# Seven block products in place of eight in the MLP output product of a two-layer encoder, and narrower passes in its input product

## The chip, the cores and the metric

The kernel runs on one core of one Trainium2 chip. The metric is the device time of one execution in microseconds (us), the median of several runs. One execution was taken with the profiler.

## The reference

Two layers of an encoder over 256 tokens of width 1024, in float32. Each layer has two kinds of attention, a gated mix and an MLP. The part that matters here is the MLP:

```python
h = rms_norm(x, g_mlp_pre)
h = jnp.square(jax.nn.relu(h @ w_mlp_in)) @ w_mlp_out      # 1024 -> 4096 -> 1024
x = x + rms_norm(h, g_mlp_post)
```

## The kernel before

**Products in three passes.** A float32 product on TensorE (PE) is made of three passes: each operand is split into a high part (cast to float32r) and a low part (the rest). `high*high`, `high*low` and `low*high` are added in a PSUM bank. The weights are split in the kernel as they arrive: the scalar engine (ACT) casts a piece into `w_hi` (`hi`, line 678), the vector engine (DVE) subtracts it from the loaded data into `w_lo` (`lo`, line 1019), and PE uses both. A piece is half a load, 1024 elements per partition. Pieces live in a ring of four (`RING`): the cast of piece p waits until PE has used piece p - 4 (`piece_used`), and PE waits for `lo_ready`. The loads go through the queue of SyncE (SP) into four slots of `raw`; a slot is loaded again when DVE has split its last piece.

**The MLP.** The 4096 hidden columns are worked in 8 chunks of 512. Chunk 0's input product is `first_product`, chunk 1's `turned_product` (256-column passes, lines 1455 to 1457). From chunk 2 on it is `mlp_in_wide`, which gives the hidden columns on partitions: for each block of 128 hidden columns and each 128 rows of the weights one pass of 512 columns (high weights times high and low activations side by side in `s1_both`, line 1698) and one of 256 (low weights, line 1701). The two halves of a bank are then added by DVE (`sum_h`, `tensor_reduce`, line 1067) into `relu_h`; ACT does the relu in place (line 784); GpSimd (POOL) squares it into `tok` (`square`, line 531); ACT and DVE split that into the stationary operand `s2_hi`, `s2_lo` (lines 792 and 1058).

The output product (`mlp_out`, and `product` with lines 1380 to 1382) takes chunk j's 512 rows of `w_mlp_out` in four pieces. For each piece, token tile (2 of 128) and block of 128 rows it issues three passes of 512 columns: 48 passes per chunk. The sums of all chunks stay in the four banks `acc`, one for each token tile and half of the 1024 output columns. `finish` is the product of chunk 7, ordered by token tile so that the norm of tile 0 can start early.

**Order.** Per layer PE runs: `first_product`, `turned_product` for chunk 1, output product of chunk 0, then a loop of five (input product of chunk j + 2, output product of chunk j + 1), then the input product of chunk 7, the output product of chunk 6 and `finish`. All engines follow a hand-written program order with semaphores.

Of the kernel before, what the change touches and what calls it, by code (L numbers as in the profile page):

```python
# [65 lines left out]
    + [("out", 4, COL)] * 4 + [("mlp", 4, COL)] * 32)  # L66
NL = len(LOADS)
NP = 2 * NL
# [4 lines left out]
L_LOOP = L_MLP + 6  # L73
LOOP_J = MJ - 3
assert NL == 64 and LOADS[L_MLP][0] == "mlp" and LOADS[L_MLP - 1][0] == "out"

# [7 lines left out]
def piece_rows(p):  # L84

    nk = LOADS[p // 2][1]
    cut = (nk + 1) // 2
    return (0, cut) if p % 2 == 0 else (cut, nk)
# [77 lines left out]
def build(nc, x_d, pos_d, g_mix_pre, g_mix_post, g_mlp_pre, g_mlp_post, w_in, b_gate, sinks_d, q_norm,  # L166
          kv_norm, w_uq, w_ukv, w_oa, w_ob, w_out, w_mlp_in, w_mlp_out, out_d):
    ctx = ExitStack()
    with ctx:
# [101 lines left out]
        h_summed = sem("h_summed")  # L271
# [30 lines left out]
        def raw_view(p):  # L302

            n, N = p // 2, LOADS[p // 2][2]
            k0, k1 = piece_rows(p)
            return raw[:, n % RAW, k0 * N:k1 * N]

        def in_order(p, *views):

            if LOADS[p // 2][0] != "ukv":  # L310
                return views
# [4 lines left out]
        def split_view(buf, p):  # L316
            k0, k1 = piece_rows(p)
            return buf[:, p % RING, 0:(k1 - k0) * LOADS[p // 2][2]]
# [32 lines left out]

        h_banks = sc + tp
# [30 lines left out]
        def _(sp):  # L383
# [8 lines left out]
            def raw_free(pos, n):  # L392

                sp.wait_ge(lo_ready, pos.count(NP, 2 * n + 2, 8))
# [9 lines left out]
            for l in range(DEPTH):  # L404
# [56 lines left out]
                mlp_out(pos, n + 4, 0)  # L461
                with sp.Fori(0, LOOP_J) as j:
                    here = Pos(l, j)
                    mlp_in(here, L_LOOP, j + 2)
                    mlp_out(here, L_LOOP + 2, j + 1)
                n = L_LOOP + 4 * LOOP_J
                mlp_in(pos, n, MJ - 1)
                mlp_out(pos, n + 2, MJ - 2)
                mlp_out(pos, n + 4, MJ - 1)
                assert n + 6 == NL  # L470
# [11 lines left out]
        def _(pool):  # L482
# [41 lines left out]
            def square(pos, j):  # L524

                for t in range(TT):
                    pool.wait_ge(relu_done, pos.count(TT * MJ, TT * j + t + 1, TT))
                    if j > 1:

                        pool.wait_ge(h_split, pos.count(TT * (MJ - 1), TT * (j - 2) + t + 1, TT))  # L530
                    g.tensor_tensor(tok[:, t, 0:COL], relu_h[:, t, :], relu_h[:, t, :], ALU.mult).then_inc(h_ready, 1)  # L531
# [37 lines left out]
            for l in range(DEPTH):  # L569
# [69 lines left out]
                square(pos, 0)  # L639
                square(pos, 1)  # L640
                with pool.Fori(0, LOOP_J) as j:
                    square(Pos(l, j), 2)
                square(pos, MJ - 1)
# [6 lines left out]
        def _(act):  # L650
# [15 lines left out]
            def hi(pos, upto):  # L666

                while state[0] <= upto:
                    p = state[0]
                    n = p // 2  # L670
# [1085 lines left out]
```

## Time and profile before

| | |
|---|---|
| median of 3 runs | 753.39 us (753.14 to 753.55) |
| the profiled execution | 753.48 us |
| its span, first to last instruction | 751.5 us |
| PE, matmul busy | 740.3 us, 99% of the span |
| DVE busy | 505.8 us, 67% |
| ACT busy | 414.4 us, 55% |
| POOL busy | 158.6 us, 21% |
| HBM read | 130.59 MB, 175 GB/s over the span |

A share is an average over stages, and a matmul is counted with its pipeline, so that overlapping ones make PE look full. The distance from one start to the next tells what a pass costs. In the timeline a row gives start, duration, engine, line, operation and operands; `x2` means that two like instructions were merged, and the bracket at the end tells how long the engine was idle before it and who ended that.

### The profile page before, as it was taken

The numbers are of one execution on the slowest core, as the hardware profiler recorded it, in microseconds if no ns is written. First come the engines' busy times: TensorE is split into PE (matmuls) and PEld (weight loads), VectorE is DVE, ScalarE is ACT, GpSimd is POOL, SyncE is SP. The second block draws the span as 40 slices with busy tenths as digits, with TensorE's granted clock in tenths as the row PEclk, the third lists the DMA queues.
The fourth block names the chain that finished last, engine by engine and source line by source line (L and its number), as shares of the span: only waits on it lengthen the run. The fifth ranks groups of instructions, "written<-read, shape, count | busy, mean of one in ns | idle before, by whom it ended". The sixth has DMA issues, their size and how long they took to land.

```text
span 751.5 us, 11313 instructions
## 1 busy us (share of the span) xinstructions
PE 740.3 (99%) x4194; PEld 640.3 (85%) x4194; DVE 505.8 (67%) x678; ACT 414.4 (55%) x779; POOL 158.6 (21%) x262
## 2 busy tenths in 40 slices
PE   8999999999999999999999999999999999999996
PEld 7999887888798888888889997888888988888885
DVE  5878777567765656656686887766668566565674
ACT  6867665434664544444576866644447444554452
POOL 1990433000130111110128414220003210011110
PEclk9999999999999999999999999999999999999999
DMA  7866633565465545466338584335473656555511
GB/s 260 208 205 218 220 113 115 167 215 168 129 215 178 213 170 193 156 207 211 105 114 242 182 281 144 113 117 194 139 223 121 220 164 223 189 202 176 202 71 56
DMA packets 79501, 132.19 MB, mean 176 GB/s; under 512 B 15290, under 2 KB 21476, under 8 KB 79204
## 3 DMA queue, kind: packets, MB, share of 16 engines
q1 hardware_dynamic: 79188, 131.64, 53.7%
q8 instruction: 26, 0.43, 0.2%
q14 instruction: 15, 0.12, 0.0%
q10 hardware_dynamic: 272, 0.00, 0.0%
HBM read 130.59 MB, written 1.05 MB: 175 GB/s over the span
## 4 chain that ended last, share of the span: by engine, by line
PE 91%; DVE 3%; ACT 2%; POOL 1%; DMA 1%; issue 1%; SPq 0%; POOLq 0%; ACTq 0%; DVEq 0%
PE acc L1380 15%; PE acc L1382 15%; PE acc L1381 15%; PE tp L1698 6%; PE sc L1698 6%; PE acc L1414 4%; PE tp L1355 3%; PE tp L1701 3%; PE sc L1701 3%; PE sc L1516 2%; PE sc L1457 2%; PE sc L1455 2%; PE sc L1456 2%; PE sc L1380 2%; PE sc L1381 1%; PE sc L1382 1%
## 5 line engine op out<-in xcount | busy, mean ns | idle before, releaser
L1019 DVE TENSOR_TENSOR w_lo<-raw,w_hi 128x1024 fp32r<-128x1024 f32 (+4 forms) x256 | 306.0, 1216 | 162.5 <-ACT w_hi L678 161.0
L678 ACT CAST w_hi<-raw 128x1024 fp32r<-128x1024 f32 (+4 forms) x256 | 251.5, 997 | 177.7 <-PE acc L1382 94.3
L1380 PE MATMUL acc<-w_hi,s_hi 128*128 128x512 f32 x288 | 112.2, 390 | 0.0
L1381 PE MATMUL acc<-w_lo,s_hi 128*128 128x512 f32 x288 | 112.1, 389 | 0.0
L1382 PE MATMUL acc<-w_hi,s_lo 128*128 128x512 f32 x288 | 112.0, 389 | 0.0
L1380 PE MATMUL acc<-w_hi,s_both 128*128 128x512 f32 (+2 forms) x256 | 95.5, 373 | 0.0
L1382 PE MATMUL acc<-w_hi,s_both 128*128 128x512 f32 (+2 forms) x256 | 93.4, 365 | 0.0
L1381 PE MATMUL acc<-w_lo,s_both 128*128 128x512 f32 (+2 forms) x256 | 93.3, 364 | 0.0
L531 POOL TENSOR_TENSOR tok<-relu_h 128x512 f32<-128x512 f32 x32 | 37.0, 1161 | 263.6 <-ACT relu_h L784 241.6
L1382 PEld LDWEIGHTS acc<-w_hi,s_lo 128*128 128x128 f32 x288 | 54.1, 188 | 11.3
L1380 PEld LDWEIGHTS acc<-w_hi,s_hi 128*128 128x128 f32 x288 | 54.1, 188 | 10.8
L1381 PEld LDWEIGHTS acc<-w_lo,s_hi 128*128 128x128 f32 x288 | 54.1, 188 | 10.6
L1698 PE MATMUL tp<-s_both,w_hi 128*128 128x512 f32 x192 | 60.3, 395 | 0.0
L1698 PE MATMUL sc<-s_both,w_hi 128*128 128x512 f32 x192 | 60.2, 395 | 0.0
L802 ACT ACTIVATE probs<-sc,neg_m 128x128 f32<-128x128 f32 (+2 forms) x96 | 35.2, 390 | 40.0 <-DVE neg_m L1137 22.0
L1382 PEld LDWEIGHTS acc<-w_hi,s_both 128*128 128x128 f32 x256 | 48.2, 188 | 7.8
L1380 PEld LDWEIGHTS acc<-w_hi,s_both 128*128 128x128 f32 x256 | 48.2, 188 | 7.4 <-DVE w_lo L1019 0.4
L1381 PEld LDWEIGHTS acc<-w_lo,s_both 128*128 128x128 f32 x256 | 48.3, 189 | 6.9
L514 POOL TENSOR_TENSOR var<-sums,norm_k 128x1 f32<-128x1 f32 x24 | 8.5, 354 | 186.9 <-ACT squares L740 186.7
L1701 PEld LDWEIGHTS tp<-s_both,w_lo 128*128 128x128 f32 x192 | 36.1, 188 | 8.5
L1701 PEld LDWEIGHTS sc<-s_both,w_lo 128*128 128x128 f32 x192 | 36.1, 188 | 8.4
L784 ACT ACTIVATE relu_h<-relu_h 128x512 f32<-128x512 f32 x24 | 15.2, 632 | 44.0 <-DVE relu_h L1067 44.0
(212 smaller groups left out, 1337.6 us busy)
## 6 DMA issues: line engine op xcount, KB each, us to landing
raw<-in_w_mlp_in SPq DMA_DIRECT2D x32, 1024.0 KB, 5.3
raw<-in_w_mlp_out SPq DMA_DIRECT2D x32, 1024.0 KB, 5.0
raw<-in_w_in SPq DMA_DIRECT2D x24, 1024.0 KB, 5.3
raw<-in_w_oa SPq DMA_DIRECT2D x8, 1024.0 KB, 5.0
raw<-in_w_out SPq DMA_DIRECT2D x8, 1024.0 KB, 5.0
raw<-in_w_ob SPq DMA_DIRECT2D x4, 1024.0 KB, 4.9
raw<-in_w_in SPq DMA_DIRECT2D x3, 768.0 KB, 4.9
raw<-in_w_in SPq DMA_DIRECT2D x4, 576.0 KB, 6.5
```

Source lines behind the costliest of these rows:

```text
L531: g.tensor_tensor(tok[:, t, 0:COL], relu_h[:, t, :], relu_h[:, t, :], ALU.mult).then_inc(h_ready, 1)
L678: s.copy(high, src).then_inc(hi_ready, 1)
L784: s.activation(relu_h[:, b, :], relu_h[:, b, :], ACT.Relu).then_inc(relu_done, 1)
L802: ins = s.activation(probs[:, i % 2, a * w:(a + 1) * w], sc[i % 2][:, a * w:(a + 1) * w], ACT.Exp, bias=neg_m[:, c + a:c + a + 1], scale=S ...
L1019: v.tensor_tensor(low, src, high, ALU.subtract).then_inc(lo_ready, 1)
L1355: ins = nc.tensor.transpose(b[0:rows, i * P:(i + 1) * P], src, ident[:, :])
L1380: mm(banks[t][:, 0:N], h[:, kk, tk], wh[:, k, :], start=(start and k == 0), stop=False)
L1381: mm(banks[t][:, 0:N], h[:, kk, tk], wl[:, k, :], start=False, stop=False)
L1382: ins = mm(banks[t][:, 0:N], low[:, kk, tk], wh[:, k, :], start=False, stop=(stop and k == b - a - 1))
L1414: ins = mm(acc[t][:, 0:N], xs[:, 2 * i + k, t * P:(t + 1) * P], w[:, k, :], start=(first and i == 0 and k == 0), stop=(last and i == 3 and ...
L1698: mm(bank[:, :].rearrange("p (a n) -> p a n", a=2), wh[:, k, cols], s1_both[:, :, 2 * i + k, :], start=(i == 0 and k == 0), stop=False)
L1701: ins = mm(bank[:, SEQ:2 * SEQ], wl[:, k, cols], s1_hi[:, 2 * i + k, :], start=False, stop=(i == 3 and k == 1))
```

## The change

For chunks 1 to 6 the output product is done in the Strassen-Winograd way. A half chunk has two blocks of 128 hidden rows; with the two token tiles and the two halves of the output columns it is a product of 2 x 2 by 2 x 2 blocks, eight block products. The change makes seven, from sums of the blocks, in seven PSUM banks (`acc` 0 to 3, `sc` 0 and 1, `tp` 0), each with three passes of 512 columns.

- POOL makes the sums of the activations (`square_and_sum`: two squares of 256 elements, four sums of 128) and of the weights (`weight_sums`: a difference of 1024 elements, two of 512, into the gate buffers, two halves ahead).
- A half chunk has six weight pieces: `in0` and `in1` (1024 elements each), `low` (1024), `first` (512), `t13` and `t24` (1024 each, of the sums).
- The seven banks are combined once per layer on DVE (`add_bank`, seven additions of 512), before the output product of chunk 0, which now comes after chunks 1 to 6. Chunk 7 stays last.
- The input product of chunks 2 to 7 goes in blocks of 128 hidden columns (`in_piece`), 24 passes of 256 columns each, all three kinds of pass into the same 256 columns of a bank; the relu reads that bank (`relu_of`), so `sum_h` goes away. Its loads have rows of 256 columns, those of the output weights whole rows of 1024.
- The loops over chunks are written out.

```diff
-    + [("out", 4, COL)] * 4 + [("mlp", 4, COL)] * 32)
+    + [("out", 4, COL)] * 4 + [("mlp", 4, COL)] * 4 + [("in", KD, SEQ), ("pair", 2, D)] * 12 + [("mlp", 4, COL)] * 4)
...
+def half_order(s):
+    if s == 0:
+        return ("in0", "in1", "low", "first", "t13", "t24")
+    if s == NHALF - 1:
+        return ("in0", "low", "first", "t13", "t24", "in1")
+    return ("in0", "low", "first", "in1", "t13", "t24")
...
             def raw_free(pos, n):
-                sp.wait_ge(lo_ready, pos.count(NP, 2 * n + 2, 8))
+                upto = LAST_PIECE[n - RAW] + 1 - (NP if n < RAW else 0)
+                sp.wait_ge(lo_ready, pos.count(NP, 2 * RAW + upto))
...
+            def relu_ready(pos, j, b):
+                if j < 2:
+                    pool.wait_ge(relu_done, pos.count(2 * TT, TT * j + b + 1))
+                else:
+                    pool.wait_ge(h_relued, pos.count(2 * NHALF, 2 * (2 * (j - 2) + b) + 2))
+                if j > 1:
+                    pool.wait_ge(h_split, pos.count(TT * (MJ - 1), TT * (j - 2) + b + 1))
+            def square_and_sum(pos, j, b):
+                relu_ready(pos, j, b)
+                tile = tok[:, b, :].rearrange("p (s n) -> p s n", n=P)
+                ka = relu_h[:, b, 0:SEQ].rearrange("p (t n) -> p t n", t=TT)[:, ::-1, :]
+                kb = relu_h[:, b, SEQ:2 * SEQ].rearrange("p (t n) -> p t n", t=TT)
+                g.tensor_tensor(tile[:, 0:2, :], ka, ka, ALU.mult)
+                sums_a.link(g.tensor_tensor(tile[:, 2:4, :], kb, kb, ALU.mult))
+                g.tensor_tensor(tile[:, 7, :], tile[:, 1, :], tile[:, 0, :], ALU.subtract)
+                sums_a.link(g.tensor_tensor(tile[:, 5, :], tile[:, 0, :], tile[:, 3, :], ALU.add))
+                sums_a.link(g.tensor_tensor(tile[:, 6, :], tile[:, 5, :], tile[:, 1, :], ALU.subtract))
+                g.tensor_tensor(tile[:, 4, :], tile[:, 2, :], tile[:, 6, :], ALU.subtract).then_inc(h_ready, 1)
+            def weight_sums(pos, s):
+                n = L_PAIR + 2 * s + 1
+                loads, in_layer = transfers(n)
+                pool.wait_ge(raw_full[n % RAW], pos.count(16 * in_layer, 16 * loads))
+                if s >= 2:
+                    pool.wait_ge(lo_ready, pos.count(NP, 2 * RAW + half_piece(s - 2, "t24") + 1))
+                block = raw[:, n % RAW, :].rearrange("p (i n) -> p i n", i=4)
+                made = t_buf[s % 2].rearrange("p (i n) -> p i n", i=4)
+                at = lambda i: pos.count(3 * NHALF, 3 * s + i)
+                g.tensor_tensor(made[:, 0:2, :], block[:, 1::2, :], block[:, 0:2, :], ALU.subtract).then_inc(t_made, 1)
+                pool.wait_ge(t_made, at(1))
+                g.tensor_tensor(made[:, 2, :], block[:, 3, :], made[:, 0, :], ALU.subtract).then_inc(t_made, 1)
+                pool.wait_ge(t_made, at(2))
+                g.tensor_tensor(made[:, 3, :], block[:, 2, :], made[:, 2, :], ALU.subtract).then_inc(t_made, 1)
...
+                for t in range(TT):
+                    square(pos, 0, t)
+                sums_a.pos, sums_a.n = pos, 0
+                weight_sums(pos, 0)
+                for b in range(2):
+                    square_and_sum(pos, 1, b)
+                weight_sums(pos, 1)
+                for s in range(NHALF):
+                    j, b = half_of(s)
+                    if j < MJ - 1:
+                        square_and_sum(pos, j, b)
+                    else:
+                        square(pos, j, b)
+                    if s + 2 < NHALF:
+                        weight_sums(pos, s + 2)
...
+                    elif part in ("t13", "t24"):
+                        act.wait_ge(t_made, pos.count(3 * NHALF, 3 * ((n - L_PAIR) // 2) + (1 if part == "t13" else 3)))
...
+            def relu_of(pos, s, f):
+                j, b = half_of(s)
+                used(pos, half_piece(s, f"in{f}"))
+                act.wait_ge(h_ready, pos.count(TT * MJ, TT * (j - 1) + b + 1))
+                nc.scalar.activation(relu_h[:, b, f * SEQ:(f + 1) * SEQ], in_bank(s, f)[:, 0:SEQ], ACT.Relu).then_inc(h_relued, 1)
...
+                for half in range(1, NHALF - 1):
+                    p = P_PAIR + 6 * half
+                    relu_of(pos, half, 0)
+                    hi(pos, p + 4)
+                    pair_high(pos, *half_of(half - 1))
+                    hi(pos, p + 6)
+                    relu_of(pos, half, 1)
+                    hi(pos, p + 9)
...
-            def sum_h(pos, j, p):
...
+            def pair_low(pos, j, b):
+                dve.wait_ge(h_hi, pos.count(TT * (MJ - 1), TT * (j - 1) + b + 1))
+                v.tensor_tensor(pair_lo[b], tok[:, b, P:D], pair_hi[b].bitcast(F32), ALU.subtract).then_inc(h_split, 1)
...
+                for half in range(1, NHALF - 1):
+                    p = P_PAIR + 6 * half
+                    lo(pos, p + 4)
+                    pair_low(pos, *half_of(half - 1))
+                    lo(pos, p + 6)
+                    lo(pos, p + 9)
...
+                def in_piece(pos, s, f):
+                    p, bank = half_piece(s, f"in{f}"), in_bank(s, f)
+                    pe.wait_ge(lo_ready, pos.count(NP, 2 * RAW + p + 1))
+                    if s > 0:
+                        pe.wait_ge(h_relued, pos.count(2 * NHALF, 2 * s + f))
...
+                    for k in range(KD):
+                        mm(out, wh[:, k, :], s1_hi[:, k, :], start=(k == 0), stop=False)
+                        mm(out, wh[:, k, :], s1_lo[:, k, :], start=False, stop=False)
+                        ins = mm(out, wl[:, k, :], s1_hi[:, k, :], start=False, stop=(k == KD - 1))
+                    ins.then_inc(piece_used, 1)
...
+                for half in range(1, NHALF - 1):
+                    in_piece(pos, half, 0)
+                    pair_low(pos, half)
+                    pair_first(pos, half)
+                    in_piece(pos, half, 1)
+                    pair_t13(pos, half)
+                    pair_t24(pos, half)
...
+                def whole(c):
+                    return lambda t: pe.wait_ge(combined, pos.count(7, (1, 4, 6, 7)[2 * c + t]))
+                for i in range(4):
+                    product(pos, P_LAST + i, 0, s2, pair[i // 2], free=whole(i // 2) if i % 2 == 0 else None, seeded=True)
```

## Rows read from the trace of the kernel before

**Rows 1.** Page: busy per engine; granted clock in 40 slices; the chain by engine.

```profile
PE 740.3 (99%) x4194; PEld 640.3 (85%) x4194; DVE 505.8 (67%) x678; ACT 414.4 (55%) x779; POOL 158.6 (21%) x262
...
PEclk9999999999999999999999999999999999999999
...
PE 91%; DVE 3%; ACT 2%; POOL 1%; DMA 1%; issue 1%; SPq 0%; POOLq 0%; ACTq 0%; DVEq 0%
```

**Rows 2.** Timeline of PE: start us, duration us, the starts that bound the products.

```profile
222.89 0.40 PE L1380 MATMUL acc<-w_hi,s_hi 128*128 128x512 f32 x1
...
233.80 0.39 PE L1698 MATMUL sc<-s_both,w_hi 128*128 128x512 f32 x1
...
244.94 0.40 PE L1380 MATMUL acc<-w_hi,s_hi 128*128 128x512 f32 x1
...
365.96 0.39 PE L1380 MATMUL acc<-w_hi,s_hi 128*128 128x512 f32 x1
```

**Rows 3.** Timeline of PE: first and last of runs without a gap.

```profile
210.51 0.28 PE L1455 MATMUL sc<-s_both,w_hi 128*128 128x256 f32 x1
...
216.15 0.28 PE L1457 MATMUL sc<-s_both,w_lo 128*128 128x256 f32 x1
...
228.13 0.39 PE L1382 MATMUL acc<-w_hi,s_lo 128*128 128x512 f32 x1
```

**Rows 4.** Timeline of DVE: three low parts back to back.

```profile
209.13 3.50 DVE L1019 TENSOR_TENSOR w_lo<-raw,w_hi 128x1024 fp32r<-128x1024 f32 x3 [1.95 <-ACT w_hi L678]
```

**Rows 5.** ACT in 222 to 372 by shape (busy us, mean ns), and one timeline row.

```profile
L678 ACT CAST w_hi<-raw 128x1024 fp32r<-128x1024 f32 x53 | 55.0, 1049 | 51.8 <-PE acc L1382 26.8 <-PE tp L1701 25.0
L792 ACT CAST s_hi<-tok 128x512 fp32r<-128x512 f32 x14 | 8.0, 616 | 0.0
...
223.09 1.09 ACT L778 ACTIVATE relu_h<-sc 128x512 f32<-128x512 f32 x2 [1.78 <-PE sc L1457]
```

**Rows 6.** Single lines of POOL: duration ns min/median/max, first and last start, forms.

```profile
L531 POOL TENSOR_TENSOR tok<-relu_h x32: 1041/1042/2022, 211.6 to 727.2; 128x512 f32<-128x512 f32 x32
...
L590 POOL TENSOR_TENSOR latent<-latent,rstd x8: 616/1070/1591, 29.4 to 401.3; 128x384 f32<-128x384 f32 x4, 128x256 f32<-128x256 f32 x4
...
L600 POOL TENSOR_TENSOR gate_a<-cost,rstd x4: 395/402/1386, 37.8 to 403.5; 128x128 f32<-128x128 f32 x4
```

**Rows 7.** Timeline of DVE and POOL where low parts meet squares.

```profile
211.41 1.22 DVE L1019 TENSOR_TENSOR w_lo<-raw,w_hi 128x1024 fp32r<-128x1024 f32 x1
...
211.56 1.96 POOL L531 TENSOR_TENSOR tok<-relu_h 128x512 f32<-128x512 f32 x1 [2.31 <-ACT relu_h L778]
...
212.95 1.66 DVE L1019 TENSOR_TENSOR w_lo<-raw,w_hi 128x1024 fp32r<-128x1024 f32 x1 [0.32 <-ACT w_hi L678]
...
213.49 2.02 POOL L531 TENSOR_TENSOR tok<-relu_h 128x512 f32<-128x512 f32 x1
...
214.73 1.85 DVE L1019 TENSOR_TENSOR w_lo<-raw,w_hi 128x1024 fp32r<-128x1024 f32 x1
...
224.77 1.04 POOL L531 TENSOR_TENSOR tok<-relu_h 128x512 f32<-128x512 f32 x1
...
225.15 1.74 DVE L1019 TENSOR_TENSOR w_lo<-raw,w_hi 128x1024 fp32r<-128x1024 f32 x1 [2.58 <-ACT w_hi L678]
```

**Rows 8.** DVE with one operand in PSUM: beside a square, and a line's durations.

```profile
247.03 0.68 DVE L1067 TENSOR_REDUCE relu_h<-tp 128x256 f32<-128x512 f32 x1
...
247.35 1.04 POOL L531 TENSOR_TENSOR tok<-relu_h 128x512 f32<-128x512 f32 x1 [21.54 <-ACT relu_h L784]
...
L1111 DVE TENSOR_TENSOR s_lo<-acc,s_hi x8: 668/680/695, 101.1 to 488.5; 128x512 fp32r<-128x512 f32 x8
```

**Rows 9.** Window of an output product: length, PE, PEld, DVE, ACT, POOL busy, clock.

```profile
244.90:256.00 11.10, 11.10 (x51) 9.22 (x50) 7.28 (x8) 5.27 (x6) 2.08 (x2) 1.00 0.49 182
```

**Rows 10.** Page, DMA issues: count, KB each, median us from issue to landing.

```profile
raw<-in_w_mlp_in SPq DMA_DIRECT2D x32, 1024.0 KB, 5.3
...
raw<-in_w_in SPq DMA_DIRECT2D x4, 512.0 KB, 4.2
```

More of the change, by code:

```diff
@@ L270, in build @@
         relu_done = sem("relu_done")
-        h_summed = sem("h_summed")
+        h_relued = sem("h_relued")
+        h_step = sem("h_step")
+        t_made = sem("t_made")
+        p1_copied = sem("p1_copied")
+        combined = sem("combined")
         h_ready = sem("h_ready")
@@ L302, in raw_view @@
         def raw_view(p):
-            n, N = p // 2, LOADS[p // 2][2]
+            n, part = PIECES[p]
+            kind, nk, N = LOADS[n]
+            if kind == "in":
+                cols = slice(0, P) if part == "in0" else slice(P, 2 * P)
+                return raw[:, n % RAW, :].rearrange("p (k n) -> p k n", k=KD)[:, :, cols]
+            if kind == "pair":
+                s = (n - L_PAIR) // 2
+                return {"low": raw[:, n % RAW, D:2 * D], "first": raw[:, n % RAW, 0:COL],
+                        "t13": t_buf[s % 2][:, 0:D], "t24": t_buf[s % 2][:, D:2 * D]}[part]
             k0, k1 = piece_rows(p)
@@ L1705, in h_is_split @@
-                def h_is_split(pos, j):
-                    pe.wait_ge(h_split, pos.count(TT * (MJ - 1), TT * j, TT))
-                def mlp_out(pos, p, start=False):
-                    for i in range(4):
-                        product(pos, p + i, 0, s2, pair[i // 2], start and i % 2 == 0)
+                def in_piece(pos, s, f):
[3 more added lines that the diff above has]
+                        pe.wait_ge(h_relued, pos.count(2 * NHALF, 2 * s + f))
+                    wh, wl = (split_view(w, p).rearrange("p (k n) -> p k n", k=KD) for w in (w_hi, w_lo))
+                    out = bank[:, 0:SEQ]
+                    for k in range(KD):
[3 more added lines that the diff above has]
+                    ins.then_inc(piece_used, 1)
@@ new lines, in pair_piece @@
+                def pair_piece(pos, s, name, terms):
+                    p, b = half_piece(s, name), s % 2
+                    pe.wait_ge(lo_ready, pos.count(NP, 2 * RAW + p + 1))
+                    wh, wl = (split_view(w, p).rearrange("p (i n) -> p i n", n=COL) for w in (w_hi, w_lo))
+                    first, last = s == 0, s == NHALF - 1
+                    for i, (a, bank) in enumerate(terms):
+                        tk = slice(SUM_A[a] * P, (SUM_A[a] + 1) * P)
+                        mm(bank[:, :], pair_hi[b][:, tk], wh[:, i, :], start=first, stop=False)
+                        mm(bank[:, :], pair_hi[b][:, tk], wl[:, i, :], start=False, stop=False)
+                        ins = mm(bank[:, :], pair_lo[b][:, tk], wh[:, i, :], start=False, stop=last)
+                    ins.then_inc(piece_used, 1)
@@ new lines, in pair_low, with pair_first, pair_t13, pair_t24 @@
+                def pair_low(pos, s):
+                    pe.wait_ge(h_split, pos.count(TT * (MJ - 1), s + 1))
+                    pair_piece(pos, s, "low", (("a12", acc[0]), ("s4", acc[2])))
+                def pair_first(pos, s):
+                    pair_piece(pos, s, "first", (("a11", sc[0]),))
+                def pair_t13(pos, s):
+                    pair_piece(pos, s, "t13", (("s1", acc[3]), ("s3", tp[0])))
+                def pair_t24(pos, s):
+                    pair_piece(pos, s, "t24", (("s2", sc[1]), ("a22", acc[1])))
```

274 lines of the change are left out of this document (144 added, 130 removed).

## The prediction

> **What bounds the kernel now.** I read the page's busy shares, its chain and the clock row first, then the timeline of the MLP stage. PE is busy for 99% of the span at full granted clock, and 91% of the chain that ended last is PE [rows 1]. So the MLP stage has no slack on PE. I mark it off by two starts in the first layer: the last input product of chunk 1 ends where the first 512-column pass of the output product starts, at 222.89, and `finish`, the output product of chunk 7, starts at 365.96 [rows 2]. Between them lie 143.1 us, all PE. The profiled execution took 753.48 us (its span is 751.5), against a median of 753.39 for the runs, so I add differences to 753.4.
>
> **PE, pass by pass.** A 512-column pass follows the last after 0.227 us (228.13 to 233.80, 25 steps) and a 256-column pass after 0.120 us (210.51 to 216.15, 47 steps) [rows 2, 3]. The narrow pass costs 6.5 ns more than half a wide one. The input product of a chunk is now 32 passes of 512 and 32 of 256, 32 x 0.227 + 32 x 0.120 = 11.1 us (233.80 to 244.94 in the trace [rows 2]). After the change it is 96 passes of 256: 11.52 us, 0.38 more. The output product of a half chunk drops from 24 passes to 21, which gives 3 x 0.227 = 0.68. Over 6 chunks (12 halves) and two layers: 24 x 0.68 = 16.3 gained, 12 x 0.38 = 4.6 lost, net 11.7 us on PE alone. A half (input and output product of 256 hidden columns) then costs PE 48 x 0.120 + 21 x 0.227 = 10.5 us, where half a chunk costs 11.0 now.
>
> The Trainium skill (TensorE: Matmul & The Clock Gate, section "Wait — 56ns, not 53.3ns?") gives back-to-back passes a fixed 2.5 ns over their columns at 2.4 GHz; the rows have 13.5. By the page the narrow passes would cost almost nothing and the gain on PE would be about 14.5 us; the measured pitches decide.
>
> **What the other engines must do for it.** Per half, DVE now has 4 low parts of 1024 elements, one low part of h (512) and two reductions out of PSUM. After: five low parts of 1024 (`in0`, `in1`, `low`, `t13`, `t24`), one of 512 (`first`), and `pair_low` with 896. All seven read two SBUF operands. Back to back a 1024 costs 1.14 (three in 3.50, the last one 1.22 long) [rows 4], so DVE needs 5 x 1.14 + 0.61 + 1.0 = 7.3 us of a half. ACT casts a piece in 1.05 and 512 elements in 0.62 [rows 5]; five pieces, `first`, 896 elements of h and two relus of 256 (0.4 each, an estimate from the 1.09 of two relus of 512) make 7.6. Both are below 10.5, and by themselves would stay hidden.
>
> POOL squares 512 elements per half now (1.04 us). After the change it squares 2 x 256, makes four sums of 128 for the activations, and for the weights a difference of 1024 and two of 512. Its durations alone are 1.04 for 512, 0.62 for 256 and 0.40 for 128 [rows 6], a slope of 1.67 ns per element, so a 1024 takes 1.9. Sum: 1.9 + 2 x 1.04 + 2 x 0.62 + 4 x 0.40 = 6.8 us. Also below 10.5.
>
> **But DVE and POOL don't run side by side.** This is the step that decides. In [rows 7] a POOL square that takes 1.04 alone took 1.96 and 2.02 while DVE made low parts, and the low parts, 1.22 alone, took 1.66 and 1.85. Read the ends: DVE 212.63, POOL 213.52, DVE 214.61, POOL 215.51, DVE 216.58. Each instruction finishes a fixed time after the end of the other engine's: 0.90 for the POOL 512, 1.08 for the DVE 1024. One pair takes 1.98 us, the sum of both. The row at 225.15 says it again: DVE waits for the POOL square to end at 225.81 and ends 1.08 later. DVE instructions that read one SBUF operand and PSUM don't wait: the reduction at 247.03 keeps its 0.68 while POOL keeps its 1.04 [rows 8]. That is why the loop of before never shows it: POOL's squares fall beside the reductions there, and POOL is busy only 2.08 us per chunk [rows 9].
>
> No row has a POOL subtraction of this size beside a DVE low part. I count all nine of POOL's, because its multiplications of other shapes and operands stretched in the same way, the 0.62 to as much as 1.59 and the 0.40 to 1.39 [rows 6]. If only the two squares counted, the shared time of a half would be under 8 us; that is rival (a).
>
> The Trainium skill (SBUF — State Buffer, section "Who interferes with whom") says that a DVE instruction with two SBUF inputs and any GpSimd instruction that reads SBUF exclude each other for the whole instruction. By that rule all nine count; no run here shows it for them yet.
>
> **The sum of a half.** Held by DVE: 5 x 1.08 + 0.55 + 0.95 = 6.9. Held by POOL, 0.90 for 512 with the same slope: 1024 1.75, two 512 1.80, two 256 0.95, four 128 1.04, together 5.5. That is 12.4 us if one always follows the other at once. The upper bound is both engines' stand-alone times end to end, 7.3 + 6.8 = 14.1; the lower one gives POOL nothing but its slope, 3072 elements at 1.67 ns, 5.1, beside DVE's 6.9: 12.0. POOL's linked steps leave short holes that DVE can't always use, so I take 12.75, near the lower of the two sums because both queues have work waiting. PE's 10.5 is below all three: it will stand about 2.2 us in each half, most of it at `low` or `t13`, for `lo_ready`. The ring of four pieces lets PE run through single blockages; it can't carry a steady deficit.
>
> **A layer.** Start: after 222.89 the two first input pieces give PE 5.8 us. In that time chunk 1 must be relued (to 224.2 in the trace [rows 5]), squared and summed by POOL (2.8 alone, with waits for DVE's next pieces about 5), cast and subtracted (2 us), so `low` of half 0 starts about 3 us late. Half 1 is saturated, with its `weight_sums` behind the sums of both halves of chunk 1: 30 us for the first two halves (27 to 34). Nine more at 12.75: 114.8. The last half and the product of chunk 0 are PE again, since POOL has no weight sums left: 10.5 + 10.9, and 0.6 for handovers: 22. The seven additions of the banks are hidden: DVE takes 0.68 for 512 elements with one operand in PSUM [rows 8], and four of the seven, 2.7, must be done before tile 1 of the first piece, and the last input piece and tile 0 give them 2.9 + 1.4 us. Sum 30 + 114.8 + 22 = 166.8 against 143.1: 23.7 more, 47 for both layers. Forecast: 753.4 + 47.4 = **801 us**.
>
> **The new waits.** ACT's cast of `t13` and `t24` waits for POOL (`t_made`); behind it on ACT stand `pair_high`, the relu of `in1` and the next casts, and so DVE and PE. POOL makes these sums two halves ahead (`weight_sums(s + 2)`), so the wait costs only if POOL is a whole half late, rival (b). `relu_of` waits for `h_ready` two halves back, with the same lead. PE's wait for `h_relued` before an input piece has two or three pieces of other products in between, 1.9 us at least, against a relu of 0.4: nothing. On SP the load of the pair waits until `t24` is split, instead of being freed when its own data is read; behind it is only the next load.
>
> Transfers stay hidden. The two loads of a half have 1 KB and 4 KB rows. 512 KB in 1 KB rows lands after 4.2 us, 1 MB in 2 KB rows after 5.3 [rows 10]; even twice 4.2 and once 5.3 end to end is 13.7, with the fixed time of a transfer counted thrice, and the slot of a load is free more than a half ahead.
>
> **The rivals.** (a) *Faster: the exclusion doesn't bind.* It decides from the point where DVE and POOL together hold less than PE's 10.5. Then PE is the bound, 12 x 10.5 + 10.9 = 137 per layer, plus 1 to 3 us at the start: 743 to 748, say **745**. For it: neither engine alone is above 7.3. Against it: the lock-step ends of [rows 7], and even the lower bound of 12.0 is above 10.5. Chance 0.09. (b) *The exclusion binds, but POOL also becomes late by its own order:* each linked step waits for a whole DVE instruction, and `weight_sums` stands behind the sums of h. A half then goes to 14.1: 34 + 127 + 23 = 184 per layer, **835**. Against it: DVE has only seven instructions per half to stand in the way, and both results are needed a half later. Chance 0.11. (c) *The granted clock falls in the stalls.* It is at its full 2.4 GHz in every slice of before [rows 1], but no slice there has a stall of 2.2 us in every 13. At the other level, 1.2 GHz, the columns of a pass would take twice as long: 48 x 0.227 + 21 x 0.440 = 20.1 us for PE's half, an estimate, and some 970 in all. Chance 0.03.
>
> **How the numbers follow.** The main case has 0.75: 12.0 to 13.7 per half with 27 to 32 at the start gives 780 to 823. 0.02 is for the exclusion binding only just, near 753. The range 780 to 827 leaves out (a), (c), the case near 753 and the dearer half of (b), 0.2 together. Faster by over 0.2% 0.09, within 0.2% (1.5 us, about what can be told from no change) 0.02, slower 0.89.
>
> **What would show it.** Right: in the halves, low parts of 1.7 us and longer and POOL subtractions of twice 1.04 and longer, ends in lock step; DVE and POOL busy near 100% of the stage; PE waiting for `w_lo`; pitch of halves about 12.7. Wrong: low parts at 1.22 beside POOL, and PE dense at 10.5 per half. If PE waits for a transfer or `relu_h`, the cause is another one.

## The result and the profile after

| | before | after |
|---|---|---|
| runs, median (lowest to highest), us | 753.47 (753.14 to 753.57) | 827.84 (825.90 to 827.97) |
| profiled execution, its span, us | 753.48, 751.5 | 825.90, 824.1 |
| mean granted clock | 0.998 | 0.981 |

The ratio is 1.098, with an interval of 1.096 to 1.100. The forecast was 801 with a range of 780 to 827, so the direction and the mechanism came out, but the size did not: 74 us slower, not 47, and 0.8 above the upper end of the range. The profiled execution is the fastest of the four; the tables below are read from it.

The page of after, busy time by engine, DVE, POOL and the granted clock in tenths over 40 slices, and the chain by engine:

```profile
PE 753.7 (91%) x4506; PEld 655.9 (80%) x4506; DVE 643.7 (78%) x692; ACT 457.1 (55%) x853; POOL 450.7 (55%) x454
DVE  5778777577679798988686878766686889888994
POOL 2971421001799999994037423300039999999910
PEclk9999999999999899999999999999999899999999
PE 55%; POOL 30%; DVE 10%; ACT 3%; issue 2%; POOLq 0%; ACTq 0%; DVEq 0%
```

Against [rows 1], PE falls from 99% to 91% of the span, and the chain of work that ended last now runs through POOL for 30% and DVE for 10%; before, it was 91% PE. POOL is near full through both MLP stages, and otherwise only in one slice near the start, where it also was before. The clock row has its first 8s.

The stage of the first layer, by four starts on PE (us, duration): the first input piece of half 0, the one of half 2, the one of half 11, and the output product of chunk 7. The last column is the idle time before and who ended it:

```profile
222.55 0.28 PE L1844 MATMUL tp<-s_both,w_hi 128*128 128x256 f32 x1
253.54 0.39 PE L1844 MATMUL tp<-s_both,w_hi 128*128 128x256 f32 x1 [0.57 <-DVE w_lo L1149]
379.87 0.39 PE L1844 MATMUL tp<-s_both,w_hi 128*128 128x256 f32 x1 [0.57 <-DVE w_lo L1149]
402.00 0.39 PE L1524 MATMUL acc<-w_hi,yb_hi 128*128 128x512 f32 x1
```

It lasts 179.45 us, where [rows 2] had 143.07 (365.96 - 222.89). That is 36.4 more, and twice that, 72.8, is the whole difference of the spans (72.6). So nothing outside the two MLP stages moved: from the start of chunk 7's product in the first layer to the start of the stage in the second it is 225.62 us in both traces. Inside, by the terms of the prediction:

| term, per layer | forecast | measured |
|---|---|---|
| first two halves | 30 | 31.0 |
| nine halves, each | 12.75 | 14.04 (126.33 in all) |
| last half and the product of chunk 0 | 22 | 22.1 |

The nine halves alone hold the miss: 9 x 1.29 x 2 = 23 us of the 27.

The two windows below are those nine halves and one of them (length, then busy time and count of PE, weight loads, DVE, ACT and POOL, the granted clock, the DMA share, GB/s):

```profile
253.50:379.90 126.40, 104.21 (x622) 89.70 (x622) 110.86 (x64) 63.24 (x82) 122.87 (x82) 0.96 0.47 150
337.90:351.90 14.00, 11.11 (x70) 9.53 (x70) 12.06 (x8) 6.93 (x10) 13.61 (x10) 1.00 0.47 147
```

POOL is busy for 97% of them, against 2.08 us per chunk before [rows 9], and PE for 82%. The waits of the same stretch put it down to the low parts, with no transfer among them (engine, line, waited for: us in total, times, longest):

```profile
PEld sc L1858 <- DVE w_lo L1149: 22.6, 9, 3.1
PE sc L1858 <- DVE w_lo L1149: 18.8, 9, 2.6
```

L1858 with `sc` is the first pass of a half that uses `low`: one stall of 2.5 us in each of the nine halves (2.1 by PE's own row), where the prediction put about 2.2 for the whole half. The half has 3.5 above PE's 10.5; most of the rest is a second, short stall before an input piece.

**The lock-step and the term that was too small.** The timeline of DVE and POOL from `t13` of one half on, start and duration:

```profile
342.39 1.33 DVE L1149 TENSOR_TENSOR w_lo<-gate_a,w_hi 128x1024 fp32r<-128x1024 f32 x1 [0.61 <-ACT w_hi L791]
342.72 1.32 POOL L614 TENSOR_TENSOR tok<-tok 128x128 f32<-128x128 f32 x1
344.01 2.42 POOL L627 TENSOR_TENSOR gate_b<-raw 128x1024 f32<-128x1024 f32 x1
345.05 2.32 DVE L1186 TENSOR_TENSOR s_lo<-tok,s_hi 128x896 fp32r<-128x896 f32 x1 [1.33 <-ACT s_hi L905]
346.50 2.00 POOL L629 TENSOR_TENSOR gate_b<-raw,gate_b 128x512 f32<-128x512 f32 x1
347.30 2.28 DVE L1149 TENSOR_TENSOR w_lo<-gate_a,w_hi 128x1024 fp32r<-128x1024 f32 x1
348.58 2.15 POOL L631 TENSOR_TENSOR gate_b<-raw,gate_b 128x512 f32<-128x512 f32 x1
349.50 2.31 DVE L1149 TENSOR_TENSOR w_lo<-raw,w_hi 128x1024 fp32r<-128x1024 f32 x1
350.69 1.59 POOL L609 TENSOR_TENSOR tok<-relu_h 128x256 f32<-128x256 f32 x1
```

Add start and duration and read the ends in order: DVE 343.72, POOL 344.04, POOL 346.43, DVE 347.37, POOL 348.50, DVE 349.58, POOL 350.73, DVE 351.81. Each ends a fixed time after the end before it, whoever had it: 1.08 for a DVE 1024 as forecast, 0.95 for `pair_low`; for POOL 0.32 for a 128, 2.39 for the 1024 (`weight_sums`, its difference of the raw blocks) and 1.13 to 1.15 for a 512. The forecast had 1.75 for that 1024 and 0.90 for a 512. Over the whole half, which ends 14.01 us after the last, DVE holds 6.9 (forecast 6.9) and POOL 7.1 (forecast 5.5). Their sum is the half: 14.0. No hole is left but the 0.08 us between two linked steps of POOL where DVE has nothing to do.

The POOL 1024 takes 2.42 from its start, with no DVE instruction in its way (DVE's next one, at 345.05, is the one that waits), where the slope taken from [rows 6] gave 1.9. All the instructions behind that slope read one tensor twice, or one tensor and a broadcast factor. Here the two operands are different data.

### The profile page after: what moved, and what is told of

It is laid out like the page before. It is cut to its first block, busy times and chain, and to the rows that moved or that the text cites. A ratio compares the mean times of both kernels' runs of the same rounds, so it can differ in the third digit from the quotient of the medians.

```text
span 824.1 us, 11845 instructions
## 1 busy us (share of the span) xinstructions
PE 753.7 (91%) x4506; PEld 655.9 (80%) x4506; DVE 643.7 (78%) x692; ACT 457.1 (55%) x853; POOL 450.7 (55%) x454
## 4 chain that ended last, share of the span: by engine, by line
PE 55%; POOL 30%; DVE 10%; ACT 3%; issue 2%; POOLq 0%; ACTq 0%; DVEq 0%
PE acc L1524 9%; PE acc L1527 9%; PE acc L1526 8%; DVE w_lo L1149 6%; PE acc L1559 4%; POOL tok L609 3%; POOL tok L610 3%; PE tp L1499 3%; POOL tok L612 3%; POOL gate_a L627 3%; POOL gate_b L627 2%; POOL tok L614 2%; POOL tok L611 2%; POOL gate_a L631 2%; POOL gate_b L631 2%; PE sc L1661 2%
## 5 line engine op out<-in xcount | busy, mean ns | idle before, releaser
L1149 DVE TENSOR_TENSOR w_lo<-raw,w_hi 128x1024 fp32r<-128x1024 f32 (+4 forms) x256 | 336.4, 1349 | 58.7 <-ACT w_hi L791 57.1
L1844 PE MATMUL tp<-s_both,w_hi 128*128 128x256 f32 x384 | 114.8, 299 | 14.3 <-DVE w_lo L1149 14.3
L1845 PE MATMUL tp<-s_both,w_hi 128*128 128x256 f32 x384 | 112.3, 292 | 0.0
L1846 PE MATMUL tp<-s_both,w_lo 128*128 128x256 f32 x384 | 112.1, 292 | 0.0
L1844 PEld LDWEIGHTS tp<-s_both,w_hi 128*128 128x128 f32 x384 | 77.3, 201 | 23.9 <-DVE w_lo L1149 22.8
L1845 PEld LDWEIGHTS tp<-s_both,w_hi 128*128 128x128 f32 x384 | 77.6, 202 | 1.0
L1846 PEld LDWEIGHTS tp<-s_both,w_lo 128*128 128x128 f32 x384 | 77.3, 201 | 0.0
L1149 DVE TENSOR_TENSOR w_lo<-gate_a,w_hi 128x1024 fp32r<-128x1024 f32 x24 | 45.4, 1899 | 11.4 <-ACT w_hi L791 11.4
L1149 DVE TENSOR_TENSOR w_lo<-gate_b,w_hi 128x1024 fp32r<-128x1024 f32 x24 | 44.4, 1850 | 11.3 <-ACT w_hi L791 11.3
L665 POOL TENSOR_TENSOR probs<-probs,denom 128x512 f32<-128x512 f32 x26 | 28.9, 1115 | 41.8 <-DVE denom L1235 41.8
L1186 DVE TENSOR_TENSOR yb_lo<-tok,yb_hi 128x896 fp32r<-128x896 f32 x12 | 28.4, 2370 | 12.9 <-ACT yb_hi L905 12.9
L1600 PE MATMUL sc<-s_both,w_hi 128*128 128x256 f32 x128 | 36.7, 287 | 0.0
```

The lines of the kernel that those rows point to most:

```text
L1149: v.tensor_tensor(low, src, high, ALU.subtract).then_inc(lo_ready, 1)
L1600: mm(out, wh[:, k, cols], s1_hi[:, kk, :], start=(i == 0 and k == 0 and f % 2 == 0), stop=False)
L1844: mm(out, wh[:, k, :], s1_hi[:, k, :], start=(k == 0), stop=False)
L1845: mm(out, wh[:, k, :], s1_lo[:, k, :], start=False, stop=False)
L1846: ins = mm(out, wl[:, k, :], s1_hi[:, k, :], start=False, stop=(k == KD - 1))
```

## The experiments

Each is timed beside the kernel before on the same chip (medians of it 753.34 to 753.40). "Half" means the time from one `in0` to the next in the first layer, "the start" what the first two halves cost beyond twice the later ones.

**Is it the weight sums on POOL?** `e1_no_wsums` drops POOL's three differences; `t13` and `t24` are split from the raw blocks instead, so two of the seven products have the wrong factor.

```diff
-                        "t13": t_buf[s % 2][:, 0:D], "t24": t_buf[s % 2][:, D:2 * D]}[part]
+                        "t13": raw[:, n % RAW, 0:D], "t24": raw[:, n % RAW, D:2 * D]}[part]
...
-                g.tensor_tensor(made[:, 0:2, :], block[:, 1::2, :], block[:, 0:2, :], ALU.subtract).then_inc(t_made, 1)
+                g.memset(made[:, 0, 0:1], 1.0).then_inc(t_made, 1)
```
(and the other two differences likewise)

> The changed kernel without POOL's three subtractions of the weights: t13 and t24 are split from the loaded data (so these two block products are computed with the wrong weights), POOL sets one element each instead. PE, ACT and DVE do the same work as in the changed kernel. Theory (a DVE low part and a POOL instruction that reads SBUF exclude each other): DVE holds 6.9 us of a half, POOL 2.4, together 9.3, below PE's 10.5; so halves of 10.5 to 10.8 us, low parts near 1.2 where no square is in the way, 744 to 752 us. Rival 1 (the time is lost to the clock of PE or to the order of the waits, not to POOL's reads): halves stay at 12 to 14 us, over 790 us.

Measured: 753.47, ratio 0.9994 (0.9984 to 1.0003). All 74 us are gone. The window of e1 over most of its halves:

```profile
250.00:355.00 105.00, 105.00 (x687) 96.34 (x686) 83.34 (x72) 70.14 (x91) 50.22 (x80) 1.00 0.58 190
```

PE is dense, POOL at 48%, and the halves are 10.56 each, 0.06 from the forecast of PE's cost. The three instructions are the cause of the slowdown. But the total is not the theory's 744 to 752: the start costs 5.1 us per layer (halves of 14.1 and 12.1), where rival (a) gave it 1 to 3. The place, on ACT, POOL and PE of e1:

```profile
231.78 1.33 POOL L614 TENSOR_TENSOR tok<-tok 128x128 f32<-128x128 f32 x1
233.14 0.94 ACT L905 CAST s_hi<-tok 128x896 fp32r<-128x896 f32 x1 [2.31 <-POOL tok L614]
233.99 3.46 ACT L791 CAST w_hi<-raw 128x1024 fp32r<-128x1024 f32 x4
234.71 0.39 PE L1860 MATMUL acc<-w_hi,yb_lo 128*128 128x512 f32 x1
237.04 0.39 PE L1844 MATMUL tp<-s_both,w_hi 128*128 128x256 f32 x1 [1.94 <-DVE w_lo L1149]
237.61 0.41 PE L1845 MATMUL tp<-s_both,w_hi 128*128 128x256 f32 x1
237.81 0.42 PE L1846 MATMUL tp<-s_both,w_lo 128*128 128x256 f32 x1
```

ACT stands 2.31 us in `pair_high(1, 1)` for POOL's last sum of half 1. The cast of `in0` of half 1 is queued behind it, and PE waits for that piece from 234.71 to 237.04. Two more things make up the 5.1: PE stood 1.3 us before `low` of half 0 (228.57 to 230.03), and after the stall at 237.04 its clock falls. From 237.61 on 16 narrow passes follow at 0.213 us instead of 0.120, which is 1.5 us; the window from 238 to 242 has a granted clock of 0.62. The ten runs of e1 show the price of that drop: from 750.68 at a mean clock of 0.999 to 753.84 at 0.994, twice 1.5 us apart.

**Does POOL's occupation hold DVE up, or its reading?** `e2_fill_only` leaves the sums out in the same way, and POOL fills the whole sum buffer three times instead, writing without reading.

```diff
-                g.tensor_tensor(made[:, 0:2, :], block[:, 1::2, :], block[:, 0:2, :], ALU.subtract).then_inc(t_made, 1)
+                g.memset(t_buf[s % 2][:, 0:4 * COL], 1.0).then_inc(t_made, 1)
```
(three times)

> As e1, but POOL fills the buffer of the sums three times (2048 elements each, linked as the subtractions were) in place of the subtractions; products as in e1. POOL writes as long as before, about 5.4 us per half, and reads nothing for it. Theory, exclusion through the reads alone: fills pass beside the low parts, halves of 10.5 to 11, 744 to 758 us. Rival 2, POOL's mere occupation or its writes are what DVE waits for: 6.9 + 2.4 + 5.4 = 14.7 us per half, 830 us or more.

Measured: 759.60, ratio 1.008 (1.007 to 1.010). The timeline:

```profile
298.04 1.80 POOL L627 MEMSET gate_b<- 128x2048 f32 x1
299.10 1.09 DVE L1186 TENSOR_TENSOR s_lo<-tok,s_hi 128x896 fp32r<-128x896 f32 x1 [1.33 <-ACT s_hi L905]
299.90 1.82 POOL L629 MEMSET gate_b<- 128x2048 f32 x1
300.11 2.35 DVE L1149 TENSOR_TENSOR w_lo<-raw,w_hi 128x1024 fp32r<-128x1024 f32 x2
```

Beside the fills `pair_low` takes 1.09 and two low parts take 2.35 together, what they take alone ([rows 4]: three in 3.50). POOL is busy for 92% of the window that e1 fills to 48%, and the halves are 11.03. So it is POOL's reads that DVE can't share; POOL being busy, and its writes, cost DVE nothing. The time above e1, and the miss of the expectation by 1.6, come from POOL's queue: the squares and sums of h stand behind 5.5 us of fills, and `low` comes about half a microsecond late in each half. Nine halves of 0.47 more in two layers are 8.5 us. Against e1's run without a clock drop, 750.68, e2 (clock 0.999) is 8.9 slower; against its median 6.1.

The Trainium skill (SBUF — State Buffer, section "Who interferes with whom") has the exclusion between a DVE instruction with two SBUF inputs and a GpSimd instruction that reads SBUF. It excepts a GpSimd instruction that only writes. The traces of after and of e2 agree: ends in strict turn with reads, 1.09 beside a fill.

**Why is POOL's share 7.1, not 5.5?** `e3_forms` keeps the sizes of the three weight instructions and changes their operands: the 1024 and the last 512 subtract a tensor from itself, the middle one multiplies two different ones. The weight sums are then not those of the reference.

```diff
-                g.tensor_tensor(made[:, 0:2, :], block[:, 1::2, :], block[:, 0:2, :], ALU.subtract).then_inc(t_made, 1)
+                g.tensor_tensor(made[:, 0:2, :], block[:, 0:2, :], block[:, 0:2, :], ALU.subtract).then_inc(t_made, 1)
...
-                g.tensor_tensor(made[:, 2, :], block[:, 3, :], made[:, 0, :], ALU.subtract).then_inc(t_made, 1)
+                g.tensor_tensor(made[:, 2, :], block[:, 3, :], made[:, 0, :], ALU.mult).then_inc(t_made, 1)
...
-                g.tensor_tensor(made[:, 3, :], block[:, 2, :], made[:, 2, :], ALU.subtract).then_inc(t_made, 1)
+                g.tensor_tensor(made[:, 3, :], block[:, 2, :], block[:, 2, :], ALU.subtract).then_inc(t_made, 1)
```

> The changed kernel with other operands for POOL's three weight instructions, all of the same size and place (the sums are then wrong, and with them two of the seven products): the 1024 subtracts one tensor from itself, the first 512 multiplies two tensors in place of a subtraction, the second 512 subtracts a tensor from itself. In the changed kernel POOL is alone from 344.04 to 346.43 with the 1024, which is 2.4 us where the forecast had 1.9, and a 512 ends 1.12 to 1.15 after DVE where the forecast had 0.90. Theory A, two different SBUF tensors as inputs cost POOL more: alone or from DVE's end, the 1024 takes 1.8 to 1.9, the multiplication 1.12 to 1.15, the last 512 0.9. Theory B, subtraction is dearer than multiplication: 2.4, 0.9, 1.15. Under A the half shortens by 0.5 to 0.8 us from 14.0.

Measured, one run: 810.85, halves of 13.24 in the stretch below (13.33 on average over nine). The timeline:

```profile
325.24 1.89 POOL L627 TENSOR_TENSOR gate_a<-raw 128x1024 f32<-128x1024 f32 x1
326.29 1.80 DVE L1186 TENSOR_TENSOR yb_lo<-tok,yb_hi 128x896 fp32r<-128x896 f32 x1 [1.33 <-ACT yb_hi L905]
327.21 2.01 POOL L629 TENSOR_TENSOR gate_a<-raw,gate_a 128x512 f32<-128x512 f32 x1
328.00 2.30 DVE L1149 TENSOR_TENSOR w_lo<-gate_b,w_hi 128x1024 fp32r<-128x1024 f32 x1
329.30 1.90 POOL L631 TENSOR_TENSOR gate_a<-raw 128x512 f32<-128x512 f32 x1
```

The subtraction of 1024 with one source takes 1.89, the 1.9 of the forecast. The one with one source of 512 ends at 331.20, 0.90 after DVE's 330.30. The multiplication of two sources ends at 329.22, 1.13 after DVE's 328.09. It is two different operands that cost, not the subtraction. These are theory A's numbers. The gain of a half, 0.77, is 2.42 - 1.89 and 1.14 - 0.90.

The trace of before had a row that says so, and the forecast passed it by. POOL's groups in its first 210 us (busy, mean ns):

```profile
L377 POOL TENSOR_TENSOR tok<-tok,gate_a 128x128 f32<-128x128 f32 x2 | 0.9, 460 | 0.2
```

It is 0.46 for 128 elements of two tensors, where [rows 6] have 0.40 with a factor that is broadcast. From 0.46 and 2.42 the slope is 1.96 / 896 = 2.19 ns per element; from one source it is 1.67.

The Trainium skill (GPSIMD Engine Reference, section "Elementwise — side-by-side cycle accounting") gives about 2.6 cycles per element at 1.2 GHz for `tensor_tensor` and calls it "the two-input RD-port floor"; that is 2.17 ns. With the 0.18 us that the 128 leaves over this slope as its fixed part, the POOL 1024 would be about 2.4, an estimate, and the trace agrees with its 2.42.

**What do the narrow passes cost by themselves?** `e4_narrow_input` is the kernel before, with the input product in passes of 256 and the relu read from the bank; it leaves nothing out.

```diff
-                                mm(bank[:, :].rearrange("p (a n) -> p a n", a=2), wh[:, k, cols], s1_both[:, :, 2 * i + k, :],
-                                   start=(i == 0 and k == 0), stop=False)
+                                mm(bank[:, 0:SEQ], wh[:, k, cols], s1_hi[:, 2 * i + k, :],
+                                   start=(i == 0 and k == 0), stop=False)
+                                mm(bank[:, 0:SEQ], wh[:, k, cols], s1_lo[:, 2 * i + k, :], start=False, stop=False)
...
-                    s.activation(relu_h[:, b, :], relu_h[:, b, :], ACT.Relu).then_inc(relu_done, 1)
+                        ins = s.activation(relu_h[:, b, f * SEQ:(f + 1) * SEQ], h_banks[2 * b + f][:, 0:SEQ], ACT.Relu)
```
(DVE's sum of the bank's two halves goes)

> The kernel before with the input product of chunks 2 to 7 in 256-column passes, three for each block, into one half of each bank, and the relu reading the bank; DVE's reductions go away. The second part of the change alone; pieces, loads and the output product are as before. Nothing is left out. By the pitches each chunk costs 0.38 us more on PE: 753.4 + 12 x 0.38 = 758.0 (757 to 759.5). Rival: the banks come free earlier and the relu is off DVE, which wins something back: 753 to 755.

Measured: 758.13, ratio 1.006 (1.005 to 1.008). 4.7 us slower, and 12 x 0.38 = 4.6 was the sum. The pitches of 0.227 and 0.120 hold, and what the rival hoped to win back isn't there.

The Trainium skill (TensorE: Matmul & The Clock Gate, section "Wait — 56ns, not 53.3ns?") gives a pass a fixed 2.5 ns over its columns. By that e4 would stand within 1 us of before, an estimate (4.6 x 1.25 / 6.5 = 0.9). It stands 4.7 above, and the measurement decides.

**Can the sums be had more cheaply?** `e5_wsums_dve` moves `weight_sums` from POOL to DVE, `e6_act_squares` also the squares of nine halves from POOL to ACT. Neither leaves anything out.

```diff
                     pair_low(pos, *half_of(half - 1))
                     lo(pos, p + 6)
+                    weight_sums(pos, half + 1)
                     lo(pos, p + 9)
...
+                if 0 < s < NHALF - 2:
...
+                    nc.scalar.activation(dst, part.rearrange("p (t n) -> p t n", t=TT), ACT.Square).then_inc(h_squared, 1)
```
(the added line at the top is e5, on DVE; the other two are e6, on ACT, behind the relu)

> The changed kernel with the three subtractions of the weights moved from POOL to DVE, in DVE's order behind the first low part of the next half. Nothing is left out. Theory: DVE holds 6.9 + 1.08 + 2 x 0.55 = 9.1 us, POOL 2.4: halves of 11.5 to 11.9 us, 770 to 785 us. Rival 3, no exclusion and DVE's queue as the bound: 7.3 + 2.4 = 9.7, below PE's 10.5, 745 to 750 us.

> As e5, and the squares of nine of the twelve halves are made by ACT behind the relu instead of by POOL. Nothing is left out. Theory: DVE 9.1 + POOL 1.5 (four sums of 128) = 10.6 us beside PE's 10.5: halves of 10.7 to 11.2 us, 748 to 762 us, close to the kernel before. Rival 3 gives 745 to 750 as for e5.

Measured: e5 773.53, ratio 1.027 (1.025 to 1.029); e6 762.35, ratio 1.012 (1.010 to 1.014). The window of e5:

```profile
254.00:370.00 116.00, 110.50 (x686) 97.24 (x685) 115.24 (x105) 72.98 (x92) 56.59 (x52) 1.00 0.56 187
```

DVE is busy for 99% of it, and the halves are 11.52, as the theory had it: 9.1 us for DVE and 2.4 for POOL's reads are 11.5, and the time lies in its range. So the sum of held times gives a half for a second division of the work, this time to 0.02. In e6 the halves come out at 10.56 and 11.26 in turn, 10.87 on average. That is close to PE's cost, but the total is 0.35 above the expected range and still 9 us above before.

**Can the start be saved?** `e7_early_in` is e1 (weight sums left out) with the next half's `in0` taken up ahead of `pair_high(1, 1)` and `pair_low(1, 1)`. `e8_early_both` does the same to e6, with the weight sums of half 0 one place earlier, and leaves nothing out.

```diff
-                hi(pos, P_PAIR + 5)
+                hi(pos, P_PAIR + 6)
                 pair_high(pos, 1, 1)
...
-                lo(pos, P_PAIR + 5)
+                lo(pos, P_PAIR + 6)
                 pair_low(pos, 1, 1)
```

> As e1 (no weight sums on POOL, two products wrong), with one more step: at the start of the MLP stage ACT casts and DVE splits the input piece of half 1 before the activations of chunk 1's second half instead of behind them. In e1 PE stands from 234.7 to 237.0 for that piece, while all later halves run at 10.56 us. Theory, e1 gives its gain back at the start of the stage: 2.2 us less per layer, 749 us (748 to 750.5). Rival, the wait only moves to the next piece (the activations of half 1, or the ring): 752 to 753.5.

> As e6 (weight sums on DVE, squares on ACT, nothing left out), with the step of e7 and the weight sums of half 0 before the low parts of its first pieces instead of behind them. In e6 PE stands 3.1 us for the activations of half 0 behind those sums, then runs four us at half clock, and 1.5 us later on. Theory, start of the stage: 5 to 7 us less in all, 755 to 757.5. Rival, the start is set by POOL's sums of the activations: 760 or more.

Measured: e7 750.72, ratio 0.997 (0.995 to 0.998); e8 759.38, ratio 1.008 (1.006 to 1.010). Both are above what was expected, e7 by 0.2 and e8 by 1.9 us. In e7 the start falls from 5.1 to about 1.5 us per layer (halves of 12.0 and 11.0), but the later halves go to 10.75: `low` is 0.2 to 0.3 us late in each, and POOL is at its sums for 68 of 100 us, against 53 in e1 (246 to 346 in both). Why the same loop settles otherwise is not shown. And what e7 gains over e1 is no more than the clock drop: the trace of e7 has none there, and e1's run at a mean clock of 0.999 took 750.68, no longer than e7's 750.72. The wait itself moved on, as the rival had it. With the weight sums left out entirely, the change would gain 2.7 us.

In e8 the wait moved instead of going. The first two halves take 12.0 and 14.6. PE of e8 at `low` of half 1:

```profile
237.89 0.28 PE L1854 MATMUL tp<-s_both,w_lo 128*128 128x256 f32 x1
240.62 0.77 PE L1866 MATMUL acc<-w_hi,s_hi 128*128 128x512 f32 x1 [2.45 <-DVE w_lo L1139]
241.19 0.63 PE L1867 MATMUL acc<-w_lo,s_hi 128*128 128x512 f32 x1
241.61 0.63 PE L1868 MATMUL acc<-w_hi,s_lo 128*128 128x512 f32 x1
242.04 0.63 PE L1866 MATMUL acc<-w_hi,s_hi 128*128 128x512 f32 x1
```

PE gets no pass from 237.89 to 240.62, for a low part that stands behind the weight sums of half 1 on DVE. Then its wide passes follow at 0.43 instead of 0.23: the granted clock from 240.6 to 243.3 is 0.50, the 1.2 GHz level.

**Is it DVE's order or DVE's length?** `e10_ordered` spreads the weight sums of e8 over DVE's queue; `e9_sums_dve` moves the four activation sums of nine halves from POOL to DVE as well, so that POOL reads nothing there. Neither leaves anything out.

```diff
-                lo(pos, P_PAIR + 6)
+                lo(pos, P_PAIR + 8)
                 weight_sums(pos, 1)
...
                     lo(pos, p + 6)
-                    weight_sums(pos, half + 1)
+                    weight_sums(pos, half + 1, (0,))
+                    lo(pos, p + 8)
+                    weight_sums(pos, half + 1, (1, 2))
                     lo(pos, p + 9)
+                    if half < NHALF - 2:
+                        act_sums(pos, half)
```
(the last two lines are e9 alone)

> As e8 (weight sums on DVE, squares on ACT, early pieces; nothing left out), with DVE's order changed: the weight sums of half 1 go behind the low parts of its low and first piece, and in later halves the 1024 stays before these two pieces and the two 512 go behind them. In e8 PE stands 2.7 us in half 1 for the low part behind the sums, and its clock then drops for 3.4 us. Theory, order of DVE at the start: 2 to 3 us less per layer, halves as before (10.6 and 11.3 in turn, DVE's own length), 753.5 to 756. Rival, DVE's length decides there too and the wait moves on: 758 or more.

> As e10, and DVE makes the four sums of the activations of nine halves as well, so that POOL reads nothing in these halves. Nothing is left out. Theory: DVE has no other engine to wait for, but its own length is 5 x 1.14 + 0.61 + 1.0 + 2.65 for the weight sums + about 1.1 for the four small ones = 11.1 us, above PE's 10.5: halves near 11.1, 755 to 759 us. Rival, the small sums cost DVE less than POOL's exclusion does: halves of 10.6, 748 to 752 us.

Measured: e10 758.64, ratio 1.007 (1.005 to 1.009); e9 759.06, ratio 1.007 (1.005 to 1.009). The windows over four halves, e10, then e9:

```profile
274.00:318.00 44.00, 44.00 (x281) 39.07 (x280) 43.83 (x43) 31.94 (x47) 16.42 (x16) 1.00 0.58 192
```

```profile
274.00:318.00 44.00, 44.00 (x284) 39.56 (x283) 43.59 (x58) 32.42 (x47) 0.00 (x0) 1.00 0.60 192
```

DVE is busy for over 99% of both. It makes no difference whether POOL reads (16.42 us) or does nothing at all (0.00): the halves settle at 10.80 in both, since the sums take about as long on DVE as the port took from it. That is DVE's own length, 0.24 above the 10.56 that e1 has as PE's cost; e9's working had 11.1 for it. The time of e9 lies just above its range, and e10's where its rival put it (758 or more): DVE's length decides. The 0.7 us between the medians of e8 and e10 can't be told from their spread (758.13 to 761.31, 758.26 to 759.65). The start stays: in e10 PE waits for `in1` from 239.54 to 242.25, and its narrow passes follow at 0.21 for a while after that.

None of the versions that leave nothing out beats the kernel before.

## Why the prediction was off

**What bounds before, and PE's cost: right.** The nine halves of e1 show 10.56 where 10.5 was worked out, and e4 confirms the 4.6 us for narrow passes.

**The exclusion: right, and it decides.** It was an inference from a handful of rows beside squares; nothing in before had a POOL subtraction of that size beside a low part. Without the reads (e1, e2) the slowdown is gone or down to 6 us. With them the ends follow in turn through the half that was read, and nine halves have its length. DVE's 6.9 was exact.

**The step that failed is the term "Held by POOL ... together 5.5".** It measured 7.1, and in the working it is the part that reads "0.90 for 512 with the same slope": the slope came from squares and broadcast factors. By kind: the 1024 2.39 instead of 1.75, the two 512 2.27 instead of 1.80, the four 128 1.5 instead of 1.04 (0.32 thrice, and 0.54 for one that runs while DVE is idle), the two squares 0.94 against 0.95. With these numbers the sum of the prediction gives 6.9 + 7.1 = 14.0, and the run has 14.04. e3 shows that the operands are the reason.

**The allowance for holes and the upper bound.** The forecast put 0.35 per half on top of its 12.4 for holes; but for the 0.08 there are none. So the half missed by 1.6 for POOL less 0.3 for the holes, 1.3. And "both engines' stand-alone times end to end, 14.1" was no upper bound, since POOL's part of it rested on the same slope. That the half came out at 14.04, rival (b)'s number, is chance: (b) meant POOL late by its own linked steps. The trace has POOL at it for 97% of the time, late through the length of its instructions. The range took its top from a main case of at most 13.7 and part of (b); a price that no row showed directly should have kept more room above.

**Start and tail: the size right, with help.** 31.0 against 30, 22.1 against 22. The start of rival (a), "1 to 3 us", was too small: e1 has 5.1, because a wait of ACT for POOL's sums also holds back the next half's input piece, and because PE's clock falls behind that stall (1.5 of the 5.1). The main case didn't notice, since its 30 was an estimate for a saturated half and a late one together.

**Waits and transfers: right.** No transfer and no `t_made` wait is among the waits that PE or DVE ended last on.

**The clock, rival (c): it falls, but it doesn't decide.** One of the stretches in after where it fell:

```profile
285.00:290.00 5.00, 5.00 (x26) 4.55 (x26) 2.04 (x2) 2.94 (x4) 4.76 (x5) 0.74 0.66 197
```

The mean over the nine halves is 0.96. A slowed PE uses up the time in which it would have waited for DVE: the two halves around that place took 14.69 and 13.49, 28.2 for a pair against 28.0 elsewhere. Where PE is itself the bound, as at the start of e1, the drop is added to the time: 1.5 us per layer there, with the same drops at the start of e8 and e10. Why it falls after some stalls of 2.1 to 2.7 us and not after most stays open.

**Left open.** Why one operand read twice is cheaper for POOL than two different ones, by 0.5 ns per element, was not tried; only that it is. Nor did a run try a start without any wait.

## What to carry to other kernels

When work moves to POOL beside DVE instructions that read two SBUF operands, add what each holds; the sum is the floor of the loop, even if both engines look half idle. Take an instruction's price from a row with the same pattern of operands, not only with the same size, and if the bound sits on one such price, make the range wide on the dear side. And ask of a scheme that saves passes what it can gain at best: here PE's passes alone promised 11.7 us, and with the weight sums left out the measured gain was 2.7. The sums would have had to fit into that.

## What the runs showed of the hardware

- A POOL operation in float32 on two different SBUF operands took 0.46 us for 128 elements per partition and 2.42 for 1024; with one operand twice or broadcast 0.40 for 128 and 1.89 for 1024. For 512 elements multiplication and subtraction cost alike: 1.13 and 1.15 after DVE's end with two operands, 0.90 for both with one.
- A POOL fill of 2048 elements (1.80 us) left the DVE low part beside it at its time alone (1.09 and 2.35 for two), while beside POOL's squares, sums and subtractions the two engines' instructions ended in turn, each a fixed time after the other: 1.08 for the DVE 1024, 2.39 for the POOL 1024.
- After stalls of PE of 2.1 to 2.7 us, the granted clock was in some places at 1.2 GHz for some three microseconds: a wide pass every 0.43 us instead of 0.23 (e8), a narrow one every 0.21 instead of 0.12 (e1, e10). Runs of one kernel differed in it: e1 took 750.68 us at a mean clock of 0.999 and 753.84 at 0.994.
